# Attention with 23 and 31 key columns in place of 24 and 32, and its heads and tokens turned in other periods

## The reference, cut to what matters

```python
win_start = np.clip(qcol - kw // 2, 0, GRID_W - kw)
in_win = (kc >= win_start[..., None]) & (kc < win_start[..., None] + kw)
col_bias = jnp.where(jnp.asarray(in_win)[None, None], col_bias, NEG_INF)
...
sc = jnp.einsum('bjqhd,bkjnhd->bhjqkn', q_row, k_band).astype(jnp.float32) * scale
logits = (sc + bias[None]).reshape(b_, h, nqb, kw, kh * band)
p = jax.nn.softmax(logits, axis=-1).reshape(b_, h, nqb, kw, kh, band).astype(v.dtype)
o = jnp.einsum('bhjqkn,bkjnhd->bjqhd', p, v_band)
...
mix = head_rms_norm(jnp.concatenate([mix_a, mix_b, mix_c], axis=-1), head_norm_g[l])
x = x + mix @ w_out[l]
```

## Time and profile before

| | |
|---|---|
| Median of 3 runs | 2007.32 us (2007.18 to 2007.69) |
| Profiled execution | 2007.3 us, its span 2005.5 us |
| TensorE busy | 1981.8 us, 99% |
| VectorE busy | 1530.2 us, 76% |
| ScalarE busy | 895.3 us, 45% |
| GpSimd busy | 221.0 us, 11% |
| HBM traffic over the span | 143 GB/s |
| Attention of the first layer, scores to last values | about 199 to 280 us |

### The profile page before, as it was taken

How to read it: one execution, slowest core, us unless ns; L and a number is a source line. 1 busy time by engine, 2 the same in 40 slices (tenths; PEclk the granted TensorE clock), 3 DMA queues, 4 the chain that set the end, 5 groups by cost and what they waited for, 6 DMA issues and landing times.

```text
span 2005.5 us, 28816 instructions
## 1 busy us (share of the span) xinstructions
PE 1981.8 (99%) x10528; PEld 1647.2 (82%) x10528; DVE 1530.2 (76%) x2511; ACT 895.3 (45%) x1611; POOL 221.0 (11%) x156
## 2 busy tenths in 40 slices
PE   8999999999999999999999999999999999999998
PEld 7887788888888888888898877888888888888887
DVE  8847874799777777787777488567997777778877
ACT  7453873443333333444544549535333333344443
POOL 1221453100000000000013123630000000000000
PEclk9999999999999999999999999999999999999999
DMA  7965743124432338533477668331343233293333
GB/s 247 214 168 154 228 156 119 43 99 170 132 110 90 106 109 288 174 98 96 120 220 193 156 159 245 138 105 58 129 157 118 90 106 110 100 342 99 95 100 122
DMA packets 130988, 288.91 MB, mean 144 GB/s; under 512 B 12960, under 2 KB 17952, under 8 KB 130592
## 3 DMA queue, kind: packets, MB, share of 16 engines
q1 hardware_dynamic: 107584, 241.97, 37.0%
q0 software_dynamic: 10880, 20.97, 6.3%
q10 hardware_dynamic: 12384, 24.12, 3.4%
HBM read 227.77 MB, written 59.24 MB: 143 GB/s over the span
## 4 chain that ended last, share of the span: by engine, by line
PE 89%; DVE 6%; issue 2%; ACT 2%; DMA 0%; DVEq 0%; SPq 0%; ACTq 0%
PE bank L2249 27%; PE bank L2251 27%; PE bank L2250 27%; PE bank L2470 1%; PE bank L2398 1%; PE bank L2547 1%; DVE s_lo L1484 1%; DVE t_lo L1913 0%; PE bank L2492 0%; PE bank L2361 0%; PE bank L2485 0%; ACT logits L1189 0%; PE bank L2377 0%; DVE logits L1772 0%; DVE att_sq L1829 0%
## 5 line engine op out<-in xcount | busy, mean ns | idle before, releaser
L2249 PE MATMUL bank<-t_hi,s_hi 128*128 128x512 f32 (+1 forms) x1336 | 516.9, 387 | 0.8 <-DVE hid_cu L2026 0.5
L2250 PE MATMUL bank<-t_lo,s_hi 128*128 128x512 f32 (+1 forms) x1336 | 516.3, 386 | 0.0
L2251 PE MATMUL bank<-t_hi,s_lo 128*128 128x512 f32 (+1 forms) x1336 | 516.3, 386 | 0.0
L2249 PEld LDWEIGHTS bank<-t_hi,s_hi 128*128 128x128 f32 x1336 | 250.9, 188 | 52.4 <-DVE hid_cu L2026 1.3
L2251 PEld LDWEIGHTS bank<-t_hi,s_lo 128*128 128x128 f32 x1336 | 250.9, 188 | 50.9
L2250 PEld LDWEIGHTS bank<-t_lo,s_hi 128*128 128x128 f32 x1336 | 251.0, 188 | 50.7
L2249 PE MATMUL bank<-b_hi,s_hi 128*128 128x512 f32 x528 | 206.0, 390 | 0.1
L2251 PE MATMUL bank<-b_hi,s_lo 128*128 128x512 f32 x528 | 205.5, 389 | 0.0
L2250 PE MATMUL bank<-b_lo,s_hi 128*128 128x512 f32 x528 | 205.4, 389 | 0.0
L992 ACT ACTIVATE s_hi<-w_u 128x512 fp32r<-128x512 f32 x142 | 89.6, 631 | 233.1 <-PE bank L2251 175.6
L992 ACT ACTIVATE s_hi<-w_down 128x512 fp32r<-128x512 f32 x154 | 97.3, 632 | 201.9 <-PE bank L2251 199.9
(11 more groups left out here) (296 smaller groups left out, 3704.8 us busy)
## 6 DMA issues: line engine op xcount, KB each, us to landing
w_raw<-in_win SPq DMA_DIRECT2D x51, 512.0 KB, 5.8
w_g<-in_wg SPq DMA_DIRECT2D x44, 512.0 KB, 3.6
w_u<-in_wu SPq DMA_DIRECT2D x44, 512.0 KB, 4.5
t_raw<-hidden_t SPq DMA_DIRECT2D x88, 256.0 KB, 2.6
w_raw<-in_win POOLq DMA_DIRECT2D x40, 512.0 KB, 7.1
t_raw<-hidden_b SPq DMA_DIRECT2D x66, 256.0 KB, 2.6
hidden_b<-hid_g SPq DMA_DIRECT2D x60, 256.0 KB, 2.0
hidden_t<-hid_x SPq DMA_DIRECT2D x44, 256.0 KB, 2.0
```

The costliest lines, as they stand in the source:

```text
L2249: nc.tensor.matmul(bank, lh, rh, start=start, stop=False, skip_group_check=reopened)
L2250: nc.tensor.matmul(bank, lh, rl, start=False, stop=False, skip_group_check=reopened)
L2251: return nc.tensor.matmul(bank, ll, rh, start=False, stop=stop, skip_group_check=reopened)
```

## The change

Two things are changed. First, `KC` becomes 23, 31, 31, 24: the last column of the bands 0 to 2 is no longer among the keys of logits, bias, probabilities, transposes and values. That column is seen by no query of its tile. The scores are still computed with all columns (`KS`), and the logits read them in rows of `KS`, of which they take `KC`. Copies of turned probabilities keep their 384 columns (`NTURN`). What `load_rows` loads follows `KC`; its text is the same. Second, the order of the steps of a tile changes: `turn_heads` comes at the even period's end, `head_square` and `head_sums` in the odd period, `head_norms` at the start of the next even period, and `turn_tokens` and `tile_raw` in it; GpSimd's squares of the sums come one step earlier in its list; the tail after the last period is reordered to match. The one copy of output weights that stood in period 7 on ScalarE (`piece_hi(l, OUT_P)`) stands in period 8.

```diff
@@ -45,10 +45,12 @@
 KR = [11, 12]
-KC = [24, 32, 32, 24]
+KC = [23, 31, 31, 24]
+KS = [24, 32, 32, 24]
 CHUNK_ROWS = 4
...
 NKEY = KR[1] * KC[1]
+NTURN = NCHUNK * P
 NJ = GW // QC
@@ -273,7 +275,7 @@
         PT = nc.alloc_sbuf_tensor_at("probs_t", [P, 4 * NCHUNK, P], F32, offset=BASE + shared)
-        small[0] = shared + 4 * NKEY * 4
+        small[0] = shared + 4 * NTURN * 4
         for n, name in enumerate(("cu", "u4u", "t4")):
@@ -521,7 +523,9 @@
 
-            return B[e + 4 * (i >= SINGLE and i % 2)][:, 0:keys(i // 4)]
+            j, rr = TILES[i // 4]
+            bank = B[e + 4 * (i >= SINGLE and i % 2)]
+            return bank[:, 0:KR[rr] * KS[j]].rearrange("p (r c) -> p r c", c=KS[j])
 
@@ -876,16 +880,21 @@
                     nc.gpsimd.tensor_tensor(q_view(QL, 2 * c), q_view(QR_, 2 * c), q_view(QH, 2 * c), ALU.subtract)\
                         .then_inc(qk_lo, 1)
-                for t in range(8):
+                def sums_squared(t):
                     pool.wait_ge(p_made, l * 64 + 8 * t + 8)
                     if t:
                         pool.wait_ge(o_var, l * 8 + t)
                     nc.gpsimd.tensor_tensor(S2[:, :], SUM[:, t % 2, :], SUM[:, t % 2, :], ALU.mult).then_inc(o_eps, 1)
+
+                sums_squared(0)
+                for t in range(8):
                     pool.wait_ge(o_eps, l * 8 + t + 1)
                     pool.wait_ge(o_red, l * 8 + t + 1)
...
                     pool.wait_ge(o_var, l * 8 + t + 1)
                     nc.gpsimd.tensor_tensor(SR[:, 0:HA], SS[:, 0:HA], NHALF[:, 0:HA], ALU.pow).then_inc(o_rstd, 1)
+                    if t < 7:
+                        sums_squared(t + 1)
                     for n in {1: (0,), 5: (1,), 6: (2, 3)}.get(t, ()):
                         piece_lo(l, OUT_P + n)
@@ -1208,11 +1217,11 @@
                     if t < 2 * WHOLE:
-                        nc.scalar.activation(head_probs(t)[0:w], B[3][0:w, 0:NKEY].rearrange("p (n q) -> p n q", q=P),
+                        nc.scalar.activation(head_probs(t)[0:w], B[3][0:w, 0:NTURN].rearrange("p (n q) -> p n q", q=P),
                                              ACT.Copy).then_inc(pt_act, 1)
...
                         nc.scalar.activation(half_probs(t // 2, 1)[0:w],
-                                             B[3][0:w, 0:NKEY].rearrange("p (g q) -> p g q", q=DH),
+                                             B[3][0:w, 0:NTURN].rearrange("p (g q) -> p g q", q=DH),
                                              ACT.Copy).then_inc(pt_act, 1)
@@ -1250,27 +1259,23 @@
                         batch_hi(n)
                 for m in range(SINGLE // 2, 16):
+                    if m % 2:
+                        head_square((m - 5) // 2)
+                    if m == 8:
+                        piece_hi(l, OUT_P)
+                    turned_odd(4 * m - 1)
+                    probs(4 * m)
                     if m % 2 == 0 and m >= 6:
                         tile_raw((m - 6) // 2)
-                    if m == 7:
-                        piece_hi(l, OUT_P)
-                    if m % 2:
-                        turned_odd(4 * m - 1)
-                        probs(4 * m)
-                    else:
-                        probs(4 * m)
-                        turned_odd(4 * m - 1)
                     probs(4 * m + 1)
-                    if m % 2 == 0 and m >= 4:
-                        head_square((m - 4) // 2)
                     probs(4 * m + 2)
                     probs(4 * m + 3)
                     turned_odd(4 * m + 1)
-                tile_raw(5)
                 piece_hi(l, OUT_P + 1)
                 turned_odd(63)
+                tile_raw(5)
+                piece_hi(l, OUT_P + 2)
                 head_square(6)
-                piece_hi(l, OUT_P + 2)
                 piece_hi(l, OUT_P + 3)
                 piece_hi(l, OUT_P + 4)
...
@@ -1803,11 +1811,11 @@
                     if t < 2 * WHOLE:
-                        nc.vector.tensor_copy(head_probs(t)[0:w], B[2][0:w, 0:NKEY].rearrange("p (n q) -> p n q", q=P))\
+                        nc.vector.tensor_copy(head_probs(t)[0:w], B[2][0:w, 0:NTURN].rearrange("p (n q) -> p n q", q=P))\
                             .then_inc(pt_dve, 1)
...
                         nc.vector.tensor_copy(half_probs(t // 2, 0)[0:w],
-                                              B[2][0:w, 0:NKEY].rearrange("p (g q) -> p g q", q=DH)).then_inc(pt_dve, 1)
+                                              B[2][0:w, 0:NTURN].rearrange("p (g q) -> p g q", q=DH)).then_inc(pt_dve, 1)
 
@@ -1851,23 +1859,24 @@
                     if m % 2:
                         heads_copy((m - 3) // 2)
+                    elif m >= 6:
+                        head_norms((m - 6) // 2)
                     logits(4 * m)
                     if m % 2:
                         turned_even(4 * m - 2)
+                        head_sums((m - 5) // 2)
                         logits(4 * m + 1)
-                        head_norms((m - 5) // 2)
                     else:
                         logits(4 * m + 1)
...
                     logits(4 * m + 2)
                     logits(4 * m + 3)
-                    if m % 2 == 0:
-                        head_sums((m - 4) // 2)
                     turned_even(4 * m)
+                head_norms(5)
                 turned_even(62)
+                heads_copy(7)
                 head_sums(6)
                 head_norms(6)
-                heads_copy(7)
                 head_sums(7)
                 head_norms(7)
@@ -2396,8 +2405,8 @@
                             mm = nc.tensor.matmul(
-                                score_bank(i, e).rearrange("p (r c) -> p r c", c=KC[j]), qs[hp, c, q0:q0 + P],
-                                grid(ks[hp, c, :])[:, 4 * rr:4 * rr + KR[rr], BAND[j]:BAND[j] + KC[j]],
+                                score_bank(i, e), qs[hp, c, q0:q0 + P],
+                                grid(ks[hp, c, :])[:, 4 * rr:4 * rr + KR[rr], BAND[j]:BAND[j] + KS[j]],
                                 start=n == 0, stop=n == 2)
@@ -2575,25 +2584,26 @@
                     scores(2 * m + 1)
                     turn_halves(2 * m - 1)
+                    if m % 2 == 0 and m >= 6:
+                        turn_tokens((m - 6) // 2)
+                    values(2 * m - 2)
+                    values(2 * m - 1)
                     if m % 2 == 0:
                         turn_heads((m - 4) // 2)
-                    values(2 * m - 2)
-                    values(2 * m - 1)
-                    if m % 2:
-                        turn_tokens((m - 5) // 2)
                     turn_halves(2 * m)
                 pe.wait_ge(bt_lo, l * 8 + 8)
                 out_early(0, 0, 1)
                 turn_halves(31)
-                turn_heads(6)
+                turn_tokens(5)
                 out_early(0, 4, 5)
                 values(30)
                 values(31)
+                turn_heads(6)
                 out_early(0, 2, 3)
                 out_early(1, 0, 1)
                 turn_heads(7)
+                out_early(1, 4, 5, 2, 3)
                 turn_tokens(6)
-                out_early(1, 4, 5, 2, 3)
                 out_early(2, 0, 1, 4, 5)
                 turn_tokens(7)
```

More of the change, by code:

```diff
@@ L1770, in logits, with by_row @@
                     dve.sem_inc(dve_passed, 1)
+                    def by_row(ap):
+                        return ap.rearrange("p (r c) -> p r c", c=KC[TILES[tile][0]])
                     nc.vector.tensor_tensor_reduce(
-                        L[:, t % 4, 0:keys(tile)], score_bank(t // 2, t % 2),
-                        BIAS[BIAS_BUF[tile]][:, h // 4, h % 4 * keys(tile):(h % 4 + 1) * keys(tile)], -1.0, 3e38,
+                        by_row(L[:, t % 4, 0:keys(tile)]), score_bank(t // 2, t % 2)[:, :, 0:KC[TILES[tile][0]]],
+                        by_row(BIAS[BIAS_BUF[tile]][:, h // 4, h % 4 * keys(tile):(h % 4 + 1) * keys(tile)]), -1.0, 3e38,
                         ALU.add, ALU.min, NM[:, t % 4:t % 4 + 1]).then_inc(l_made, 1)
```

## The result

The changed kernel took 2214.19 us (median, 2213.59 to 2216.26), the kernel before in the same session 2007.47 (2007.18 to 2007.69): ratio 1.1031, 95% interval 1.1015 to 1.1048. It is slower by 207 us.

A forecast was written before the change was run, and what follows sets the result against it. TensorE, busy for almost the whole span, was taken as the bound. 2007.3 us plus 204.2 for late band loads over two layers, 3.2 for restarts and 0 for the schedule gave 2214.7, say 2215; range 2170 to 2365.

The forecast's parts named there:

- The split: Band loads of 23 and 31 rows run on one DMA engine, given 0.87; rivals with loads still spread, 0.13.
- The packet price: Time per 2 KB packet on one DMA engine: 93.4 ns chosen, bounds 80 and 147 ns.
- Step 1: Band 0's load, 368 packets from 200.5, takes 34.4 us to 234.9; `values(0)` is 26.9 us late.
- Step 2: Band 1, issued 4.8 us after `values(0)`, loads from 241.5 to 287.8; `values(8)` is 58.0 us late.
- Step 3: Band 2 queues behind 15.2 us of earlier transfers, loads from 303.0 to 349.3; `values(16)` is 102.1 us late.
- The restart: TensorE's slower first matmuls after idling: 1.6 us, added once per layer for the last stall, 3.2 us in all.
- The schedule: Moved turns in attention: 2.1 us wait gone at best, 4.0 us per layer more at worst; counted 0.
- The column: Twelve fewer columns in logits on VectorE and ScalarE save some 0.4 us per layer if all on the path.

The follow-up runs named there:

- cut loads: Changed kernel, each quarter-band `v_band` load issued as two DMAs, 16 rows and the rest, against the kernel before: 2018.19 us, ratio 1.0054.
- the order alone: Changed kernel's new order of turns with the old columns 24, 32, 32, 24, against the kernel before: 2019.04 us, ratio 1.0057.
- the 25 + 7 kernel with band 3 held back: Kernel before, loads of bands 1 and 2 cut 25 + 7 rows, band 3's load waiting until TensorE uses band 2: 2019.62 us, ratio 1.0059.

## Why the prediction was right, point by point

The time was forecast at 2215 and measured at 2214.19. The mechanism held at every step; the sizes did not all hold, and errors of opposite sign met.

*The split.* One engine for 23 and 31 rows: shown. The 0.8 us between forecast and time are luck, as the sizes below show, but the split is not. In the stands the share is 0.07 and the rate 26 GB/s, as stated (0.06, 22). The same bytes in 16 + rest rows bring back 196 us, and 23 + 1 and 31 + 1 rows without any other edit cost 207.5. By the Trainium skill, "DMA: Bandwidth & Descriptors", section "Why a DMA increments its semaphore by 16 and not by 1", the number of engines is the largest up to 16 that divides the rows, which is five for 25 rows; the trace agrees, with a share of 0.33.

*The packet price.* This term was mis-sized: 80.2 ns were measured, against 93.4 chosen. It is the lower bound from the earlier trace rows, which was the rate per engine with large rows. The Trainium skill, "SBUF — State Buffer", section "Door 1", would have given 75; the trace shows 25.5 GB/s where that page has 27.2. The row I took had all 16 engines at work, which one engine alone doesn't have. Step 1 by 80.2: 200.5 + 368 x 0.0802 = 230.0, measured 230.9 (forecast 234.9). That near fit hides two errors: the first packet went at 199.4, and most packets from 222.5 to 225.2 took about twice their time, beside a bias load.

*Step 2.* Band 1's first issue came 6.2 us after `values(0)`, not 4.8. TensorE came out of the stand at a granted clock of 0.50, which is the likely reason; it was not tested. (The bias half ahead of it has 682 KB here, not the 704 that were counted, worth under 0.1 us.) Its 496 packets ran from 240.2 to 284.8 us: 44.6 us where 39.8 were needed at 80.2 ns, and the 4.8 us lie where the biases' and the residual's transfers run beside them at 378 GB/s. `values(8)` began 1.3 us behind the last packet, at 286.08; 287.8 was forecast, so 1.7 us too much.

*Step 3.* The backlog is there, in the order and of the size that was stated: 15.2 us were forecast between bands 1 and 2, and band 2's first packet went at 300.0, 15.2 us after band 1's end at 284.8 (303.0 was forecast). Not foreseen was that SyncE's issues would be held up, and that transfers on the other engines would slow the band's packets. Band 2 ran 43.6 us, 3.8 more than its packets need. `values(16)` came 97.1 us late, 102.1 forecast.

*The restart.* 1.6 us a layer were counted at an unchanged grant. The rows show another thing: 0.50 granted until about 235.9, 290.5 and 348.5 us, that is for 4.2 to 5.0 us of work after each of the three stands, then 1.00. 24 matmuls of `values` take 2.83 us there and 1.62 before, 1.2 us more. Little of this reached the path: from `values(16)` to the first output product the changed kernel took 30.4 us (344.31 to 374.73), and the same order with cut loads, without stands, 29.7 (248.51 to 278.26). The last restart so cost 0.7 us a layer and not 1.6.

*The schedule.* Counted 0, bounds -5 to +8; alone it measures +11.7 us, outside the bounds. The step that failed is that the wait of `turn_tokens` would go at best and the odd period would be no worse. The wait did go from the pairs, but the odd period got both VectorE's sum and its copy ahead of the second logits (pairs of 8.87 and 8.90 us, 8.22 and 8.18 before), and the tail got a wait of 1.8 us. In the changed kernel, landmarks behind `values(16)` show 5.2 us a layer (102.3 - 97.1). Of these 0.7 are the restart's and 4.5 the order's: 2.0 in the pairs (29.7 with cut loads against 27.7 before, 247.19 to 274.90) and 2.5 in the tail. What the order costs before `values(16)`, 1.3 us a layer with cut loads (248.51 against 247.19), adds nothing in the changed kernel, where TensorE stands there for the loads anyway. In two layers the stands were over-estimated by 10.0 us and the restart by 1.8, and the order was under-estimated by 9.0: 2214.7 - 10.0 - 1.8 + 9.0 = 2211.9. The profiled execution took 2213.7; the 1.8 us between are the second layer's, which lost 104.1 us (206.4 - 102.3) and not 102.3.

*The column.* 0.4 us a layer was forecast. 0.85 us in all between the order alone and the whole change with cut loads is of that size, but in the old order no gain was measured (ratio 1.0014).

## What to carry to other kernels

A constant that trims work on one engine may also be the row count of a transfer. Before such a count is changed, factor it: 24 rows run on 12 engines, 25 on 5, 23 and 31 on one, and at 25.5 GB/s per engine a load that had been free sets the time of the whole kernel. If the odd count is wanted, cut the DMA so that its larger part has 16 rows.

When bounding a reordering, list for each period what each engine has before the instruction that the next engine waits for, not only the period's totals; here totals were unchanged and 11.7 us were lost.

## What the runs showed that I had not expected

- Issuing is not free behind a transfer on one engine: SyncE's four issues of band 1 took 25.0 us, against 3.7 for eight spread ones in the kernel with only band 2 cut 31 + 1.
- A transfer issued later slows an unfinished earlier one of the same queue: holding back band 3 moved band 2's landing from 286.2 to 279.6 us. On one engine the later bias packets waited behind the band's, and the band's own packets took about twice as long while the other 15 engines worked.
- After each stand TensorE's granted clock was 0.50, the lower of its two levels (1.2 GHz), and 4.2 to 5.0 us of work later 1.00 again (the window from 289 to 292 has 0.75 as a mean over both). A stand of 4.0 us was enough: in the 25 + 7 kernel with band 3 held back, the two us behind it are

```profile
252.00:254.00 2.00, 2.00 (x22) 1.85 (x18) 0.00 (x0) 0.00 (x0) 0.00 (x0) 0.50 0.02 2
```
